# Wider first halves, padded state products, and V's first products in another order, in a two-layer encoder step on one core

## The reference, cut to what matters

```
h  = ssd_mixer(x)           # layer 0: x @ w_in, causal conv, SSD scan over chunks, gated norm, @ w_out
x  = layer_norm(ALPHA*x + h, ln1[0])
x  = layer_norm(ALPHA*x + square(relu(x @ w1)) @ w2, ln2[0])       # 1024 -> 4096 -> 1024
u, v = split(gelu(x @ cm_w_in + b))      # layer 1: gated MLP mixer
v  = layer_norm(v); s = w_s (masked) applied within blocks of 128 tokens
x  = layer_norm(ALPHA*x + (u * s) @ cm_w_out, ln1[1])
x  = layer_norm(ALPHA*x + square(relu(x @ w1)) @ w2, ln2[1])
```

```
y  = (C B^T * decay) @ (x*dt)  +  decay * C h        # inside the chunk, and from the state
h  = h * exp(a_last) + B^T @ (x*dt*window)
```

## Time and profile before

| | us |
|---|---|
| median of three runs | 1685.97 |
| the profiled execution's own time | 1686.04 |
| its span, first to last instruction | 1684.3 |
| PE busy (share) | 1666.2 (99%) |
| DVE busy | 925.8 (55%) |
| POOL busy | 696.3 (41%) |
| ACT busy | 526.4 (31%) |
| granted TensorE clock, share of full | 0.997 |

### The profile page before, as it was taken

The page is one execution under the profiler, slowest core; times in us unless marked ns, Lnnn a source line. Parts: engine busy times, 40 slices in busy tenths (PEclk is TensorE's granted clock), DMA queues, the critical chain, the costliest instruction groups (busy, mean ns, idle before and its releaser), DMA issues.

```text
span 1684.3 us, 31332 instructions
## 1 busy us (share of the span) xinstructions
PE 1666.2 (99%) x12242; PEld 1619.5 (96%) x12242; DVE 925.8 (55%) x1716; ACT 526.4 (31%) x883; POOL 696.3 (41%) x577
## 2 busy tenths in 40 slices
PE   9999999999999999999999999999999999999996
PEld 9999999999999999999999888999999999999996
DVE  7789999999856441312216724887265431313226
ACT  4555545565214330312202502211024321303105
POOL 0000000000456665555555365554556655555652
PEclk9999999999999999999999999999999999999998
DMA  5223333223222222222222323222222222222222
GB/s 196 77 98 101 101 101 100 89 76 101 84 88 76 83 80 88 78 85 88 77 85 89 121 79 100 82 70 70 82 88 76 79 83 88 77 86 88 77 86 69
DMA packets 44454, 149.16 MB, mean 89 GB/s; under 512 B 5057, under 2 KB 10817, under 8 KB 43073
## 3 DMA queue, kind: packets, MB, share of 16 engines
q1 hardware_dynamic: 37888, 129.98, 23.9%
q10 hardware_dynamic: 6464, 17.74, 3.4%
HBM read 142.55 MB, written 5.15 MB: 88 GB/s over the span
## 4 chain that ended last, share of the span: by engine, by line
PE 97%; DVE 1%; ACT 1%; DMA 0%; issue 0%; ACTq 0%; DVEq 0%
PE ps L645 79%; PE ps L912 2%; PE ps L913 2%; PE ps L914 2%; PE ps L631 2%; PE ps L633 2%; PE ps L632 2%; PE ps L813 1%; PE ps L797 1%; PE ps L804 1%; PE ps L791 1%; PE ps L789 1%; PE ps L966 1%; DMA xr<-x 0%; PE ps L967 0%
## 5 line engine op out<-in xcount | busy, mean ns | idle before, releaser
L645 PE MATMUL ps<-h,wh 128*128 128x288 f32 x2944 | 505.6, 293 | 0.0
L553 POOL TENSOR_TENSOR wl<-wraw,wh 128x1024 fp32r<-128x1024 f32 x184 | 448.1, 2435 | 15.4
L645 PEld LDWEIGHTS ps<-h,wh 128*128 128x128 f32 x2944 | 427.0, 188 | 1.5 <-issue 0.4
L550 POOL TENSOR_TENSOR tick<-tick 128x1 f32<-128x1 f32 x184 | 44.5, 242 | 907.5 <-DMA wraw<-wstream 475.1
L645 PE MATMUL ps<-xh,wh 128*128 128x288 f32 x1888 | 409.2, 298 | 0.6 <-DVE r L1690 0.6
L645 PE MATMUL ps<-xl,wh 128*128 128x288 f32 x1888 | 406.6, 296 | 0.0
L645 PE MATMUL ps<-xh,wl 128*128 128x288 f32 x1888 | 405.9, 296 | 0.0
L645 PE MATMUL ps<-h,wl 128*128 128x288 f32 x1472 | 311.1, 293 | 0.0
L645 PEld LDWEIGHTS ps<-xh,wh 128*128 128x128 f32 x1888 | 304.6, 189 | 2.1 <-issue 2.0
L645 PEld LDWEIGHTS ps<-xh,wl 128*128 128x128 f32 x1888 | 305.6, 189 | 0.0
L645 PEld LDWEIGHTS ps<-xl,wh 128*128 128x128 f32 x1888 | 304.8, 189 | 0.0
(11 more groups left out here) (255 smaller groups left out, 2001.4 us busy)
## 6 DMA issues: line engine op xcount, KB each, us to landing
wraw<-wstream SPq DMA_DIRECT2D x240, 512.0 KB, 3.4
acb<-acum_scratch ACTq DMA_DIRECT2D x8, 1152.0 KB, 6.0
out_y<-r SPq DMA_DIRECT2D x8, 288.0 KB, 2.3
xr<-x ACTq DMA_DIRECT2D x4, 288.0 KB, 6.3
xr<-x SPq DMA_DIRECT2D x4, 288.0 KB, 6.6
hs<-ssm_in ACTq DMA_DIRECT2D x8, 128.0 KB, 6.0
out_ssm_s<-hsn ACTq DMA_DIRECT2D x8, 128.0 KB, 6.0
out_ssm_p<-hp ACTq DMA_DIRECT2D x8, 128.0 KB, 1.9
```

The costliest lines, as they stand in the source:

```text
L550: pool.tensor_tensor(m.tick[:, 1:2], m.tick[:, 0:1], m.tick[:, 0:1], ALU.add)
L553: pool.tensor_tensor(m.wl[:, s], m.wraw[:, s], m.wh[:, s], ALU.subtract).then_inc(S.w_ready, 1)
L645: last = mm(m.ps[:, 2 * s + h, 0:moving.shape[-1]], part, moving, start=(k, n) == (0, 0), stop=(k, n) == (KT - 1, 2))
```

## The change

- The products with the extension columns take 290 columns in both halves: the first half is columns 0 to 289, the second 288 to 577 (`ext_even`). Columns 288 and 289 are computed twice. `first_unit` keeps `ext_half`.
- In the SSD groups the chunk of 64 tokens gets tiles of its own, `xdt1` and `xw1`, whose lower 64 rows are zero; `state_product` and `intra` use all 128 rows for every chunk. Four memsets on DVE, before the first units, clear them and the lower halves of `btok` and `dec`.
- `mean_squares` runs its two parts outside and the two halves inside.
- V's first block runs, for each slice k, all five tiles with hi·hi, then with hi·lo, then with lo·hi. It waits for `xn_hi` (ACT's rounded tile), and for `xn_lo` only ahead of the third. In the later blocks the two middle units run tiles in pairs.
- In the norm before V, POOL waits for the last sum of squares ahead of V's first unit, and for the variance ahead of V's second.
- DVE's `residual_first` of tile 0 of the mixer's output stands before the last `uv_low`, that of tile 1 behind it.

```diff
+def ext_even(t, k, h):
+
+    return t[:, k, h * HT:h * HT + TX - HT]
...
+def chunk_x(m, n):
+
+    return (m.xdt1, m.xw1) if n == 1 else (m.xdt[:, n % 2], m.xw[:, n % 2])
...
         square_b6(n, u0 - 8)
+        if n == 1:
+            pool.wait_ge(S.sum2_ready, 10 * n + 10)
         split_one(u0 + 2)
+        if n == 1:
+            pool.wait_ge(S.d_var, 2 * n + 2)
         split_one(u0 + 3)
...
-        q, k = cols(n)[1], n % 2
-        mm(state_out(m, n), m.btok[0:q, k, :], m.xw[0:q, k, :].rearrange("p (h d) -> p h d", d=HD), start=True, stop=True)
+        xw = chunk_x(m, n)[1]
+        mm(state_out(m, n), m.btok[:, n % 2, :], xw[:, :].rearrange("p (h d) -> p h d", d=HD), start=True, stop=True)
...
-            last = mm(yb[p * HD:(p + 1) * HD, j * Q:j * Q + q], m.xdt[0:q, k, e * HD:(e + 1) * HD],
-                      m.dec[0:q, k, e, 0:q], start=True, stop=True)
+            last = mm(yb[p * HD:(p + 1) * HD, j * Q:j * Q + q], xdt[:, e * HD:(e + 1) * HD],
+                      m.dec[:, k, e, 0:q], start=True, stop=True)
...
-        for h in range(2):
-            for j, part in enumerate((m.sq_parts[:, 1], m.sq_parts[:, 0])):
+        for j, part in enumerate((m.sq_parts[:, 1], m.sq_parts[:, 0])):
+            for h in range(2):
...
-        run_few(u0 + 1, 3, m.xh_ext, m.xl_ext, ext_half)
-        run(u0 + 4, 3, m.xh_ext, m.xl_ext, ext_half)
+        run_few(u0 + 1, 3, m.xh_ext, m.xl_ext, ext_even)
+        run(u0 + 4, 3, m.xh_ext, m.xl_ext, ext_even)
...
         for k in range(KT):
-            pe.wait_ge(S.xn_lo, k + 1)
+            pe.wait_ge(S.xn_hi, k + 1)
             pe.wait_ge(S.w_ready, U_V + k // 2 + 1)
...
+            for part in range(3):
+                if part == 2:
+                    pe.wait_ge(S.xn_lo, k + 1)
...
+                    elif part == 2 and t < 4 and k == KT - 1:
+                        last.then_inc(S.v_done, 1)
...
+    dve.memset(m.xdt1[:, :], 0.0).then_inc(S.raw_zero, 1)
+    dve.memset(m.xw1[:, :], 0.0).then_inc(S.raw_zero, 1)
+    dve.memset(m.btok[TS:P, 1, :], 0.0).then_inc(S.raw_zero, 1)
+    dve.memset(m.dec[TS:P, 1, :, 0:TS], 0.0).then_inc(S.raw_zero, 1)
+    dve.wait_ge(S.raw_zero, 5)
...
+        if k == 15:
+            residual_first(U_CMOUT, 0, 0, x=(m.hh, m.hl))
         uv_low(k)
```

More of the change, by code:

```diff
@@ L343, in __init__ @@
         self.ones_r = put("ones_r", [P, P], F32R, offset=l0 + 14 * T * 4 + 16 * Q)
+        self.xdt1 = put("xdt1", [P, HPG * HD], offset=l0 + 14 * T * 4 + 20 * Q)
+        self.xw1 = put("xw1", [P, HPG * HD], offset=l0 + 14 * T * 4 + 28 * Q)
         self.sq_parts = put("sq_parts", [P, 2, T], F32R, offset=y0)
@@ L809, in intra @@
         q, k = cols(n)[1], n % 2
+        xdt = chunk_x(m, n)[0]
         yb = m.ps[:, 5 if n == 1 else 6, :]
@@ L898, in ffn, with v_part, v_products, v_pair @@
             elif b > 1:
-                run(u0 + 8 * b, 2, m.xh_ext, m.xl_ext, ext_half)
+                run(u0 + 8 * b, 2, m.xh_ext, m.xl_ext, ext_even)
     ffn(0, U_FFN0)
     first_unit(1, U_E)
-    run_few(U_E + 1, EARLY - 1, m.xh_ext, m.xl_ext, ext_half)
-    def v_products(t, kp, kk):
+    run_few(U_E + 1, EARLY - 1, m.xh_ext, m.xl_ext, ext_even)
+    def v_part(t, kp, kk, part):
         n = TS if t == 4 else P
         s, k = (U_V + kp) % RING, 2 * kp + kk
[L909 to L914, removed]
+        x, w = ((m.hh, m.wh), (m.hh, m.wl), (m.hl, m.wh))[part]
+        return mm(m.ps[0:n, V_BANK[t], :], x[:, k, t * P:t * P + n], w[:, s, kk * 512:kk * 512 + 512],
+                  start=(k, part) == (0, 0), stop=(k, part) == (KT - 1, 2))
+    def v_products(t, kp, kk):
+        for part in range(3):
+            last = v_part(t, kp, kk, part)
+        return last
+    def v_pair(t, kp):
+        for kk in range(2):
+            for part in range(3):
+                v_part(t, kp, kk, part)
+                v_part(t + 1, kp, kk, part)
     def v_tail(kp, kk):
@@ L931, in v_first @@
         for k in range(KT):
-            pe.wait_ge(S.xn_lo, k + 1)
+            pe.wait_ge(S.xn_hi, k + 1)
             pe.wait_ge(S.w_ready, U_V + k // 2 + 1)
[L934 to L941, removed]
+            for part in range(3):
+                if part == 2:
+                    pe.wait_ge(S.xn_lo, k + 1)
+                for t in (1, 2, 3, 4, 0) if k == 0 else range(NTOK):
+                    if (k, part, t) == (0, 0, 0):
+                        pe.wait_ge(m.slot_evac[U_E % 2], slot_turn(U_E) + 1)
+                    last = v_part(t, k // 2, k % 2, part)
+                    if part == 2 and t == 4 and k % 2:
+                        last.then_inc(S.gemm_done, 1)
+                    elif part == 2 and t < 4 and k == KT - 1:
+                        last.then_inc(S.v_done, 1)
     def v_block(b):
@@ L946, in v_block @@
             pe.wait_ge(S.w_ready, 4 * b + (U_V + kp + 1))
-            for t in range(NTOK):
+            if kp in (1, 2):
+                v_pair(0, kp)
+                v_pair(2, kp)
+            for t in ((4,) if kp in (1, 2) else range(NTOK)):
                 if kp == 0:
@@ L1523, in conv @@
             wait(dve, S.silu_ready, 4 * g)
-            dve.wait_ge(S.raw_zero, 1)
         ts(a, r[:, 0:CONV], m.cpar[:, j, 0:1], m.cpar[:, j, 4:5], ALU.mult, ALU.add).then_inc(S.conv_tap, 1)
@@ L1604, in operands @@
         xt = b[0:q, 2 * P:4 * P].rearrange("p (h d) -> p h d", d=HD)
-        tt(m.xdt[0:q, k, :].rearrange("p (h d) -> p h d", d=HD), xt, spread(m.gdt[0:q, c, :], HD), ALU.mult)
+        xdt, xw = chunk_x(m, n)
+        tt(xdt[0:q, :].rearrange("p (h d) -> p h d", d=HD), xt, spread(m.gdt[0:q, c, :], HD), ALU.mult)
         dve.wait_ge(S.dtw_ready, g + 1)
-        tt(m.xw[0:q, k, :].rearrange("p (h d) -> p h d", d=HD), xt, spread(m.dtw[0:q, c, :], HD),
+        tt(xw[0:q, :].rearrange("p (h d) -> p h d", d=HD), xt, spread(m.dtw[0:q, c, :], HD),
            ALU.mult).then_inc(S.xw_ready, 1)
@@ L1773, in block @@
         if kind == "first":
-            with dve.Fori(0, 4) as i:
+            with dve.Fori(1, 4) as i:
                 residual_first(u0, i, 0, x=(m.hh, m.hl))
@@ L2150, in vector_program @@
             rows_shifted(k // 7)
+    residual_first(U_CMOUT, 0, 1, x=(m.hh, m.hl))
     block(U_CMOUT, "first")
```

## The result

The changed kernel takes 1695.65 us (median; 1695.55 to 1695.68), the kernel before 1685.98 beside it: 1.0057 times as long, 95% interval 1.0045 to 1.0069. Forecast were 1681.0, with a range from 1671.5 to 1685.3. The forecast was wrong in its sign; what came is the third rival (the new units hand a slower pace to those behind them), with the price that it was given, and on top of it very nearly the pace that the second rival had for the units themselves (135.0 ns for its 135.1).

What follows compares the result with a forecast made beforehand. PE, busy 99% of the span, was taken as the bound. Padded products -3.8, V -0.1, residual -0.7 and even halves -0.4 summed to -5.0 us, so 1681.0 us from about 1686; range 1671.5 to 1685.3.

Steps and rivals of the forecast that it cites:

- the third rival: FFN second-matrix units: new units ahead hand on 133.33 ns, some 58 units lose 9.3 us, total 1690.3; chance 0.10.
- the second rival: Extension-column units take the 135.1 ns distance of units on x, SSD gain stays: 1685.5 us, no change; chance 0.13.
- the even halves: Extension-column units, 290 columns in both halves: 133.6 ns per matmul for 133.75, -0.4 us; bounds -8.9 and +4.1.
- the order of the sums of squares: Same matmuls in another order: 0, with 1.3 us either way if the pace of eight units behind changes.
- the eight units hold 130.0: FFN second-matrix units keep 130.0 ns behind units at 133.75; argued against the slower hand-over.
- The distance of the units on x: Upper bound for even halves: 14.3 ns above the columns, so 135.1 ns per matmul, +4.1 us.
- The padded products: SSD groups, 128 rows for every chunk: 0.48 us less per group, 8 groups, -3.8 us; bounds -2.6 and -5.0.
- V with POOL's waits: Norm before V and V's first block: about 1.0 us earlier, 0.8 to 0.9 given back; net -0.1 us, from -1.7 to +0.5.
- the second wait's collision: Norm before V: POOL's delayed second subtraction blocks DVE's product of mean and deviation until 932.3; of 2.2 us only 0.85 arrive.
- The residual: Mixer's end: PE's 0.6 us wait for DVE's residual goes, -0.7 us with the signal; bounds -0.8 and 0.
- The memsets: Four on DVE before the evacuation PE needs: under 1 us in all, covered by 1.27 us; if not, 0.3.
- The first rival: Extension-column units with equal halves fall into the FFN second matrix's even pace, 130.8 ns: 1672.5 us; chance 0.27.

Runs made afterwards that it cites:

- experiment 1: Changed kernel with only the even halves undone (288 and 290 columns again): 1682.70 us, ratio 0.998.
- experiment 2: Kernel before with even halves of 290 columns as its only edit: 1699.13 us, ratio 1.0077.
- experiment 5: Changed kernel with 288 and 290 columns in every fourth looped extension-column unit, including the last before each second matrix: 1685.71 us, ratio 0.9998.
- experiment 14: Kernel of experiment 8 with 290 and 290 columns in every fourth looped extension-column unit, including the last before each second matrix: 1690.60 us, ratio 1.0028.
- experiment 8: Kernel of experiment 4 with the last slice of V's first block tile by tile again: 1680.50 us, ratio 0.9967.
- experiment 11: Kernel of experiment 8 without both of POOL's new waits: 1681.25 us, ratio 0.9972.
- experiment 3: Kernel before with the sums of squares reordered (parts outside, halves inside) as its only edit: 1687.29 us, ratio 1.0007.
- experiment 7: Kernel before with the padded products (own tiles for the 64-token chunk, four memsets) as its only edit: 1681.89 us, ratio 0.9975.
- experiment 12: Kernel of experiment 8 without POOL's second wait, for the variance; the first stays: 1680.15 us, ratio 0.9965.
- experiment 4: Changed kernel with the even halves and the order of the sums of squares both undone: 1681.41 us, ratio 0.9973.

## Why the prediction was wrong

The measured time is 14.7 us above the forecast. Two steps failed, and one term at 0 came out at its bound: 9.3 us are the hand-over, which the sum put at nothing, 4.1 are the pace of the even halves themselves, and 1.3 the order of the sums of squares.

**The hand-over** was seen and set aside. The third rival had the mechanism, the 58 units and 9.3 us; the trace after has 9.3, and experiments 1, 2, 5 and 14 show it from both sides. (The 58 are right by luck: the six units left out are not the first of each run, but those at the ends that are run half by half.) It was given 0.10 with the argument that the eight units hold 130.0 with units at 133.75 ahead, "so they need not take over what precedes". That argument answers another mechanism: they don't take over the pace of those units, but have one of two patterns of their own, which the unit ahead picks. The row that could have warned is in the prediction itself: the same form of matmul at 130.0 and at 133.33. Where one instruction has two speeds in one trace and neither the form nor the clock tells them apart, what ran ahead is one of the few things left (the place of the operands is another), and an edit of just that deserved more.

**Even halves.** The prediction took 133.6 ns from the first unit's 22 distances, "the width that now stands everywhere", and they became 135.0. The width alone doesn't make the pace. The row has the right width, but another sequence: the first unit goes half by half, on one bank, with weights in the order hi, hi, lo; the others go from bank to bank, with hi four times and lo twice. No run shows that this is the reason, and the row isn't a fixed pace either. The same 22 distances of this unit, in which nothing was edited, take 135.0 in experiment 2:

```profile
934.16 0.30 PE L637 MATMUL ps<-xl,wh 128*128 128x290 f32 x1
...
937.13 0.30 PE L638 MATMUL ps<-xh,wl 128*128 128x290 f32 x1
```

They take 134.1 in the changed kernel and in experiment 8, and 135.0 in experiment 11. First and last of 8, then of 11:

```profile
922.82 0.30 PE L648 MATMUL ps<-xl,wh 128*128 128x290 f32 x1
...
925.77 0.29 PE L649 MATMUL ps<-xh,wl 128*128 128x290 f32 x1
```

```profile
923.26 0.30 PE L644 MATMUL ps<-xl,wh 128*128 128x290 f32 x1
...
926.23 0.30 PE L645 MATMUL ps<-xh,wl 128*128 128x290 f32 x1
```

The matmuls of 11 are those of 8 in the same order; only POOL's waits differ, and with them how long PE waited just ahead of this unit. So one row of a pace that can be entered in more than one way was taken for a price. The distance of the units on x, taken as the upper bound, came nearest: +4.1 was the bound, and 3.7 the loss; no run shows that the two have the same cause.

**The sums of squares** were priced at 0 with 1.3 either way; +1.27, the upper bound, came (experiment 3).

**What was right.** The padded products: -3.8 predicted, -4.1 measured alone (experiment 7), with the starts of rows 4 to 6 moving to where they were put. V with POOL's waits: -0.1 predicted, 0.0 measured, by the ways named: the sum set free, the second wait's collision (1.46 for 0.76), the fifth matmul waiting for the bank, and 0.9 us given back at the block's end (experiments 8, 11, 12). The residual: -0.7 predicted, -0.8 measured (45.16 us for 45.94 in the seven units). The memsets: nothing (the first run of units begins at 20.81 us for 20.83). So the sum without the even halves and the order of the sums was right to 0.1 (experiment 4). That it is so close is luck: -4.1, 0.0 and -0.8 make -4.9, and the 0.3 behind PE's last matmul, which nobody priced, brings it back to -4.6. A third wait that the change touches was not counted beside the two: PE's 0.4 us at L663 for the very sum (L1786) that POOL's subtraction lay on. It is gone too, and makes V's fifth matmul no earlier, since that waits for its bank. Two figures of the prediction don't follow from its own words: 1.5 us from 5 x 0.23 us before the block's end make the second block 0.35 late and not 0.8 to 0.9 (PE's wait for gelu was 0.67); and the first rival's time was 1672.5, not the 1671.5 at the end of the range. The first rival, equal halves falling into the even pace, was the opposite of what equal halves did.

**What stays open** is how the entry picks the pattern. Shown is that the kind of the unit of 48 matmuls ahead decides, and that mixing only its last 24 or 6 isn't enough. The last distances before the border don't tell the two apart: they are 133, 135 before and 134, 137 after, but in experiment 14, where the run has the slow pattern, 134 or 135, 135. Not shown is whether it is the phase between weight loads and matmuls, and why neither a repeated matmul nor unequal pairs bring the mixer's run to 130.0. That 24 matmuls failed may be their number, or the phase that they ended in; the runs don't tell these apart. The first unit in experiments 8 and 11 points to the moment of entry: with the same matmuls and other waits ahead, the pace was another.

## What to carry to other kernels

When one form of instruction shows two paces in one trace, treat every edit ahead of the faster stretch as an edit of that stretch, and price it at the whole stretch: here 9.3 us hung on units that cost 3.7 themselves. Test such an edit by itself, and read its neighbours' windows too, not only its own; bundled with good edits (-4.6 us here) it makes them look bad. A pace measured at the same width counts as evidence only if the order of weights and moving tiles is the same as well, and if it has been seen behind more than one entry: the row that was relied on here had 133.6, 134.1 and 135.0 without an edit of its own.

## What the runs showed of the hardware that was not expected

A run of 288 to 672 matmuls of 128x128 by 288 columns in the second matrices, the eight units and the mixer's last units, at a granted clock of 1.00, has one of two steady patterns: 132/128 in turn (or 131/129; mean 130.0 ns) or 131/131/132/140 (mean 133.3 ns). It is reached within 2 to 16 matmuls and not changed by borders of units. In the units with the extension columns more columns cost more than their share: pairs of 288/290 are 133.75 apart, 290/290 135.0, and 292/290 136.0, that is 13.3, 14.2 and 14.7 ns above the columns at 2.4 GHz. The width doesn't order the paces of different runs: the units on x, with 288/288, are at 134.3.

It is not only DVE's instructions with two tiles in SBUF that took longer beside POOL. The maximum, which reads one, took 1.28 us under POOL's subtraction, 0.92 under its rounding (experiment 12) and 0.46 beside no work of POOL.
